# Separate split-weight buffers for three first blocks, and first-tile work of two blocks ahead of the second tile

## The reference

```python
for i in range(DEPTH):                                    # DEPTH = 2
    mod = (silu(c) @ ada_w[i] + ada_b[i])[:, None, :]
    sh1, sc1, g1, sh2, sc2, g2 = jnp.split(mod, 6, axis=-1)
    h = rms_norm(x, norm_mix_g[i]) * (1 + sc1) + sh1
    y = gla_mixer(h, ...) if i % 2 == 0 else moba_mixer(h, ...)
    x = x + g1 * y
    h = rms_norm(x, norm_mlp_g[i]) * (1 + sc2) + sh2
    x = x + g2 * (jnp.square(jax.nn.relu(h @ w1)) @ w2)   # w1: 1024 x 4096, w2: 4096 x 1024
```

## Time and profile before

| | us |
|---|---|
| median of 3 runs | 657.94 |
| lowest, highest | 657.18, 659.33 |
| the profiled execution, its own time | 656.71 |
| its span, first to last instruction | 654.9 |

### The profile page before, as it was taken

The page is one execution under the profiler, slowest core; times in us unless marked ns, Lnnn a source line. Parts: engine busy times, 40 slices in busy tenths (PEclk is TensorE's granted clock), DMA queues, the critical chain, the costliest instruction groups (busy, mean ns, idle before and its releaser), DMA issues.

```text
span 654.9 us, 9235 instructions
## 1 busy us (share of the span) xinstructions
PE 618.6 (94%) x3471; PEld 516.4 (79%) x3471; DVE 474.6 (72%) x660; ACT 340.5 (52%) x581; POOL 39.4 (6%) x65
## 2 busy tenths in 40 slices
PE   4699999898999999999997999999799999999997
PEld 2457865676889988998865777788598999899985
DVE  4638997987778978979966988865787554555465
ACT  3446633547755344435538777664865543554440
POOL 3110021000000110101100000000000000000000
PEclk9799999999999999999999999999999999999999
DMA  8999599674588998999965645343357555555501
GB/s 288 353 391 393 178 365 381 212 257 153 174 313 323 374 365 313 358 364 344 355 216 182 203 131 193 130 130 129 128 191 268 188 189 192 192 192 192 192 0 65
DMA packets 58797, 156.44 MB, mean 239 GB/s; under 512 B 2786, under 2 KB 3280, under 8 KB 58768
## 3 DMA queue, kind: packets, MB, share of 16 engines
q1 hardware_dynamic: 47008, 112.41, 48.6%
q0 software_dynamic: 11760, 43.67, 18.8%
HBM read 155.02 MB, written 1.05 MB: 238 GB/s over the span
## 4 chain that ended last, share of the span: by engine, by line
PE 76%; DVE 10%; ACT 7%; issue 3%; DMA 2%; SPq 0%; ACTq 0%; DVEq 0%
PE ps L479 15%; PE ps L480 14%; PE ps L481 14%; PE ps L639 8%; PE ps L640 8%; PE ps L638 8%; DMA arena<-in_ada_w_dram 2%; DVE w_lo L1341 2%; ACT arena L1047 2%; ACT w_hi L984 1%; DVE ada_acc L1359 1%; ACT arena L1006 1%; PE ps L560 1%; DVE arena L1418 1%; ACT arena L1191 1%
## 5 line engine op out<-in xcount | busy, mean ns | idle before, releaser
L1341 DVE TENSOR_TENSOR w_lo<-w_raw,w_hi 128x1024 fp32r<-128x1024 f32 x192 | 232.6, 1222 | 121.3 <-ACT w_hi L984 121.1
L984 ACT ACTIVATE w_hi<-w_raw 128x1024 fp32r<-128x1024 f32 x192 | 201.6, 1057 | 221.5 <-PE ps L481 118.0
L479 PE MATMUL ps<-w_hi,a_hi 128*128 128x512 f32 x288 | 119.6, 415 | 15.8 <-DVE a_lo L1492 14.6
L638 PE MATMUL ps<-a_hi,w_hi 128*128 128x256 f32 x448 | 127.0, 284 | 0.0
L639 PE MATMUL ps<-a_lo,w_hi 128*128 128x256 f32 x448 | 127.0, 283 | 0.0
L640 PE MATMUL ps<-a_hi,w_lo 128*128 128x256 f32 x448 | 126.9, 283 | 0.0
L480 PE MATMUL ps<-w_lo,a_hi 128*128 128x512 f32 x288 | 113.6, 395 | 0.0
L481 PE MATMUL ps<-w_hi,a_lo 128*128 128x512 f32 x288 | 113.5, 394 | 0.0
L479 PE MATMUL ps<-w_hi,m_hi 128*128 128x512 f32 x256 | 100.2, 392 | 0.0
L480 PE MATMUL ps<-w_lo,m_hi 128*128 128x512 f32 x256 | 99.9, 390 | 0.0
L481 PE MATMUL ps<-w_hi,m_lo 128*128 128x512 f32 x256 | 99.7, 390 | 0.0
(11 more groups left out here) (187 smaller groups left out, 506.6 us busy)
## 6 DMA issues: line engine op xcount, KB each, us to landing
w_raw<-in_mlp_w_dram SPq DMA_DIRECT2D x64, 1024.0 KB, 5.6
ada_raw<-in_ada_w_dram POOLq DMA_DIRECT2D x40, 1024.0 KB, 6.5
w_raw<-in_gla_w_in_dram SPq DMA_DIRECT2D x12, 1024.0 KB, 15.7
w_raw<-in_moba_w_in_dram SPq DMA_DIRECT2D x12, 1024.0 KB, 6.7
ada_raw<-in_ada_w_dram SPq DMA_DIRECT2D x4, 1024.0 KB, 14.0
arena<-in_ada_w_dram SPq DMA_DIRECT2D x4, 1024.0 KB, 15.6
w_raw<-in_gla_w_out_dram SPq DMA_DIRECT2D x4, 1024.0 KB, 8.7
w_raw<-in_moba_w_out_dram SPq DMA_DIRECT2D x4, 1024.0 KB, 5.0
```

The costliest lines, as they stand in the source:

```text
L479: mm(out, hi, w_hi[:, slot, wc], start=first, stop=False)
L638: mm(o, w_hi[:, u, w], a_hi[:, a, :], start=u == 0 and k == 0, stop=False)
L984: A(w_hi[:, c % SPLIT], w_raw[:, c // 2, c % 2], ACT.Copy).then_inc(hi_made, 1)
L1341: V.tensor_tensor(w_lo[:, c % SPLIT], w_raw[:, c // 2, c % 2], w_hi[:, c % SPLIT].bitcast(F32), ALU.subtract).then_inc(lo_made, 1)
```

## The change

Three of the four stages are touched, v = 1, 2 and 3.

- **Own buffers.** Ten units' worth of the arena (4 K to 14 K) is given a second name, `spare`. The first block of each of the three stages has its hi and lo parts there (`unit_hi`, `unit_lo`) and no longer in `w_hi` and `w_lo`. The second block then finds the four ordinary slots free.
- **Where they are made.** A new `spare_units(v)` on ACT and on DVE makes these four units before the norm of the stage. On DVE all four `lo` of v = 2 and v = 3 stand ahead of the two `residual` calls of tile 0. For v = 1 one stands behind the first residual, one behind the third, and two behind xn of tile 0. Four units of the second block are now in `norm`: two before the first `a_lo`, one before and one after `a_lo` of the first quarter of tile 1.
- **PE.** Tile 0 of the first block, then tile 0 of the second block, with the transposes of tile 1 after its second unit (`TURN_AT = 1`), then tile 1 of the first, then tile 1 of the second. In the MLPs the second block's column groups 2 and 3 are done one tile at a time, `up_tile` and `up_rest`, as matmuls of 128 columns; groups 0 and 1 keep 256.
- **Moved pieces.** `mod_row` and `gains` have other places in the arena. In the GLA stage `second_rows` and `second_cols` stand one unit earlier on PE, and POOL's loads of `glr_w` and `glr_up` wait for `ada_pe` 6, not 4.

```diff
@@ arena
+        sb("arena_head", [P, 4 * K1])
+        spare = sb("spare", [P, 10, UNIT], F32R)
...
+        spare_hi = {v: spare[:, (0 if v == 2 else 2):(4 if v == 2 else 6)] for v in (1, 2, 3)}
+        spare_lo = {v: spare[:, (4 if v == 2 else 6):(8 if v == 2 else 10)] for v in (1, 2, 3)}
@@ POOL
-            pool.wait_ge(ada_pe, 4)
+            pool.wait_ge(ada_pe, 6)
@@ PE
+            def block_tile(v, u0, bank, tb, side={}):
+                for u in range(4):
+                    if tb == 0:
+                        pe.wait_ge(lo_made, u0 + u + 1)
+                    pe.wait_ge(a_ok, A_NORM[v] + 4 * tb + u + 1)
+                    for k in range(2):
+                        z = spare_three(ps[:, bank, :], 2 * u + k, tb, u0 + u, slice(k * COLS, (k + 1) * COLS),
+                                        u == 0 and k == 0, u == 3 and k == 1)
...
+                def up_tile(u0):
+                    pe.wait_ge(x_new, x_done(v, 1, 1))
+                    for u in range(4):
+                        pe.wait_ge(lo_made, u0 + u + 1)
+                        for c in (2, 3):
+                            part(u0, u, c, tile(0))
+                        if u == TURN_AT:
+                            turn_norm(v, 1)
+                def up_rest(u0):
+                    for us in ((0, 1), (2,), (3,)):
+                        for u in us:
+                            for c in (2, 3):
+                                part(u0, u, c, tile(1))
+                        for u in us:
+                            if u == 0:
+                                pe.wait_ge(relu_ok, 2 * m0 + 2)
+                            for c in (0, 1):
+                                z = part(u0, u, c, slice(0, SEQ))
+                            z.then_inc(unit_used, 1)
+                        if 1 in us:
+                            turn()
...
-                project_tiles(base, (0, 1), A_NORM[v], {(0, 3): lambda: turn_norm(v, 1)})
-                up(base + 4, {1: turn}, first=True)
+                block_tile(v, base, 0, 0)
+                up_tile(base + 4)
+                block_tile(v, base, 1, 1)
+                up_rest(base + 4)
...
-                first_blocks({(1, 2): lambda: second_rows(2), (2, 2): lambda: second_rows(3),
-                              (3, 0): lambda: (second_cols(2), second_cols(3)), (5, 2): glr, (6, 2): logits})
+                first_blocks({(0, 2): lambda: second_rows(2), (1, 2): lambda: (second_cols(2), second_rows(3)),
+                              (2, 0): lambda: second_cols(3), (5, 2): glr, (6, 2): logits})
...
+                block_tile(2, u0, in_bank(0, 0), 0)
+                pe.wait_ge(x_new, x_done(2, 1, 1))
+                block_tile(2, u0 + 4, in_bank(1, 0), 0, {TURN_AT: lambda: turn_norm(2, 1)})
+                block_tile(2, u0, in_bank(0, 1), 1)
+                block_tile(2, u0 + 4, in_bank(1, 1), 1, {0: lambda: after(1, 0)})
@@ ACT, norm
-                for u in range(2):
+                for u in range(4, 6):
                     hi_at(u0 + u)
-                for q in range(2):
-                    modulate_tile(v, 0, (q,))
-                    if q == 0:
-                        hi_at(u0 + 2)
-                modulate_tile(v, 0, (2, 3))
-                hi_at(u0 + 3)
+                modulate_tile(v, 0, range(4))
                 squares(v, 1)
+                for u in range(6, 8):
+                    hi_at(u0 + u)
                 modulate_tile(v, 1, range(4))
@@ DVE, lo
+                if v == 1:
+                    dve.wait_ge(o_p, 2)
+                elif v == 2:
+                    dve.wait_ge(mod_p, 3)
+                elif v == 3:
+                    dve.wait_ge(pT_p, MH)
+                    dve.wait_ge(oT_ok, 8)
@@ DVE, norm
                 scaled(v, 0)
-                for u in range(2):
+                if v == 1:
+                    spare_units(1, range(2, 4))
+                for u in range(4, 6):
                     lo_at(u0 + u)
                 low(0, 0)
...
                 scaled(v, 1)
-                for q in range(4):
+                lo_at(u0 + 6)
+                low(1, 0)
+                lo_at(u0 + 7)
+                for q in range(1, 4):
                     low(1, q)
```

## The result

| | before | after |
|---|---|---|
| median of the runs, us | 657.74 | 678.46 |
| lowest, highest | 657.18, 659.33 | 676.52, 679.96 |
| profiled execution, its own time | 656.71 | 679.39 |
| its span | 654.9 | 677.6 |

The changed kernel takes 1.0303 times the time of the one before, 95% interval 1.0284 to 1.0323. The side was forecast, the size was not: 669 in a range that ended at 674.5.

A forecast was written before the change was run, and what follows sets the result against it. PE was taken to bound nearly the whole span, with some 15 us lost at three run-ins. First MLP +4.8, MoBA +2.0, second MLP +4.2 and opening 0 gave +11.0 us on the median 657.9: 669 us, range 658 to 674.5.

The forecast's parts named there:

- the clock: Rival: the granted clock falls to half in a new PE pause, each fall losing some 2.4 us; chance 0.22.
- one fall, most likely at `turn_rot(0)`: Clock rival's single-fall case, at MoBA's first rotated block where PE waits 5 us: 671.4 us; all clock cases share chance 0.22.
- four pauses of 1.9 us and more: New PE pauses: 2.6 us in first MLP, 1.9 and 5 in MoBA, 2.9 ahead of second MLP's transposes.
- The sum at full clock: 4.8 + 2.0 + 4.2 + 0 = +11.0 us for the two MLPs, MoBA and opening, with no clock fall.
- First MLP, +4.8 forecast: First matmul at 157.6 instead of 154.44, narrow matmuls and a 1.3 us wait; end 188.0 instead of 183.21.
- MoBA, +2.0 forecast: Transposes 1.5 us later, then PE waits 5 us at `turn_rot(0)`, some 0.6 won back; bounds 0 and +3.
- Second MLP, +4.2 forecast: Four `lo` delay the residual 2.6 us; first matmul at 465.8, first `down` at 496.2 instead of 492.0.
- Opening, 0 forecast: GLA opening: earlier requests for loads against an existing wait and POOL's small loads out of the way; bounds -1.0 and +0.5.
- A price by width: Rival: the MLPs' 128-column matmuls cost 0.067 us each, not 0.11, giving 660.6 us; chance 0.13.
- A shorter run-in: Rival: four `lo` done before PE's output is ready, so all 15 us of pauses go: 652.5 us; chance 0.11.
- its own criterion: Shorter run-in's test: first `a_lo` no later than PE's last unit ends, 155.0 in the first MLP.
- PE not brought forward: Rival: tile 1 runs no sooner, pauses inside blocks stay, two more run-in waits of 5 us: 675; chance 0.04.

The follow-up runs named there:

- a_fill2: Changed kernel with extra matmuls, results overwritten, filling PE's pauses, fewer than in a first filled version; 669.4 us, ratio 1.0179.
- b_narrow: Kernel before with only column groups 2 and 3 of each MLP's second block as 128-column matmuls, old order kept; 668.3 us, ratio 1.0156.
- b_moba: Changed kernel with own buffers and new PE order kept in MoBA only, MLPs as before, opening as changed; 662.4 us, ratio 1.0068.
- b_open_new: Kernel before with the opening part of the change alone (GLA rows and columns earlier, POOL's loads later); 657.5 us, ratio 0.9993.
- best1: Own buffers, DVE's `lo` spread over its idle gaps, PE order of the kernel before in all three stages; 653.4 us, ratio 0.9943.
- a_open_back: Changed kernel with the opening part undone; 678.5 us.
- best2: best1 with one DVE residual of the first MLP moved back ahead of the wait for the output's second half; 653.5 us, ratio 0.9936.
- a_fill_lo: Changed kernel with extra matmuls only in the three waits for the last `lo` of a second block; 674.0 us, ratio 1.0257.
- a_rot: Changed kernel with `turn_rot(0)` behind the third unit of MoBA's third block instead of the first, on PE and ACT; 673.5 us, ratio 1.0223.

## Why the prediction was wrong, step by step

**The step that failed is the clock.** The forecast wrote it as a rival, "one fall, most likely at `turn_rot(0)`, gives 671.4, three give 676", gave it 0.22 with all its cases, and left it out of the sum. It had noted that the clock "stayed at full in every pause of 1.4 us", and against a fall only that "nothing in between is in the trace". In the changed kernel the clock fell five times, in or behind pauses in all three stages. The price of the falls together was about right: 7.7 us by the table, where three falls of 2.4 had been put at 7.2; they were shorter and more. What was wrong was the weight. The trace of before showed that pauses of 1.4 us, and one of 1.8, can pass at full clock, and nothing between those and the opening's, and the forecast itself had listed four pauses of 1.9 us and more.

The profiled executions add up: 22.7 us above before are 12.5 of the schedule at full clock (a_fill2), 7.7 of the dips and 2.4 of the opening.

**The sum at full clock was near.** a_fill2 has the forecast's schedule without the dips and takes 669.4 us, 11.2 more than the kernel before beside it, where 11.0 had been forecast. So close a hit is in part luck: its profiled execution is 12.5 above that of before, 1.5 more than the sum, each stage a little over its term:

- First MLP, +4.8 forecast: A +4.5, and the transposes 0.5 later from the start, +5.0. The narrow matmuls alone make 5.0 (b_narrow); the pauses won and the pauses added cancel.
- MoBA, +2.0 forecast: B +1.4 (forecast 1.5), C +1.8 (forecast 1.1), and 0.4 back from the first to the fourth `turn_rot`, +2.8. b_moba, the part by itself with its dip, is +4.2. Undersized was the way to the first rotation.
- Second MLP, +4.2 forecast: 2.5 ahead of the transposes (forecast 2.6) and 2.2 behind (forecast 1.6), +4.7.
- Opening, 0 forecast: b_open_new gives 0, between -1.7 and +0.8 us. But the start of an execution by itself moves the time by more than the term's bounds, through the clock. The forecast read the earlier trace rows, one execution, as a property of the kernel.

**The other rivals.** A price by width: out, 0.11. A shorter run-in: out in the change as made, since the first `a_lo` came 2.4 us late by its own criterion; best1 shows that the idea behind it works for about 4 us once DVE's `lo` stand in idle time and the matmuls stay wide. PE not brought forward: out, the waits between the tiles are gone. (Its 675 does not follow from its terms either: two more waits of 5 us on 669 are 679.)

**What the forecast did not see** is how little the new PE order had to win. It put the pauses that the order could remove at 5 us in each stage. The own buffers, with the hi parts out of ACT's way and with best1's DVE list, take nearly 2 of the 4.4 inside each block, with no matmul narrower. And it read all of the 14.6 us of the earlier trace rows but the opening's 3.3 as run-ins; 1.8 of them are one wait at the GLA stage's output, which the change does not touch (the matmul at 128.09 us, behind 1.77 us of idle time that ends with `a_lo`).

**How often the clock falls.** One profile of the changed kernel cannot say, but most of its pauses stand in other kernels' profiles too. Over all profiles here, the wait of 3.4 to 5.0 us at the late `turn_rot` had a dip in or just behind it seven times of seven, the pause of 2.7 ahead of the second MLP's transposes four of five, that of 2.4 ahead of the first MLP's first block four of five, and that of 1.27 for the last `lo` in an MLP six of eight. But the pause of 1.7 to 1.8 ahead of MoBA's transposes had none in six, that of 1.17 for MoBA's last `lo` none in seven, and the one of 1.77 at the GLA output none in all fourteen. Each execution has its mean granted clock as well. Time at half clock, the opening's included, estimated as (1 - mean) x 2 x span, is 28, 32, 35 and 39 us in the four executions of the changed kernel, the profiled one being the 39, and 32 to 35 in the four of a_open_back, whose profile has four of the five dips. It is 11 to 15 in a_fill2 and 6 to 20 in the executions of the kernel before that ran beside the experiments. So the dips belong to the changed kernel, and the profile shows the execution with the most of them.

**Open.** What decides whether a given pause brings the clock down: the same lists gave 31.17 and 29.82 us for stretch E in best2 and best1, and a_fill_lo lost a dip whose pause it had not touched. Length alone is not it, since 1.27 us had dips where 1.8 had none. Open too is why single executions with few dips (674.2 of a_fill2, 672.2 of a_rot) are 5 and 2.6 us longer than others with as few.

## What to carry to other kernels

A PE pause can cost more than its length. In a forecast, put the half-clock work in and behind each new pause of over 2 us into the sum as likely, and not among the rivals: here that was 7.7 us on 11, and of the pauses of 2.4 us and more in all profiles 15 of 17 had it. Between 1.2 and 1.8 us both happen, so it belongs in the range. Work that is moved earlier on a busy in-order engine should go into that engine's idle gaps, one piece at a time; as a batch ahead of a step that others wait for, it only moves the pause. And try the resource (own buffers) before the reordering: the buffers, with DVE's list fitted to its gaps, won 4 us, and the new order of PE on top cost 17, of which the narrow matmuls were 10.

## What the hardware showed that was not expected

- The clock falls in the middle of dense work, in or behind pauses of 1.3 to 4.9 us, to 0.50 for stretches of 3.4 and 6.8 us. 512-column matmuls then start every 0.43 us instead of 0.235, and eight transposes take 1.97 us instead of 1.07.
- 60 useless matmuls made the changed kernel 9.1 us faster (678.5 to 669.4).
- The opening's time at half clock differs between executions (clock 0.82 and 0.70 from 12 to 40 us in a_rot and the changed kernel, whose code is the same up to there) and moves everything behind it by 2 us and more.
- A 128-column fp32r matmul with its weight load, at full clock, has a pace of 0.11 us in runs of 24, as in the two-row sample of the earlier trace rows.
